# A ring of ten weight places in place of nine, filled in running order, and a turn of ten expert bodies in place of three

## The chip, the cores and the metric

The kernel runs on one core of one Trainium2 chip. The metric is the device time of one execution in microseconds, as the median of several runs. Three runs of the kernel before took 1612.6, 1609.94 and 1607.69 us; their median is 1609.94 us.

## The reference, cut to what matters

Two layers work on 512 tokens of 1,024 float32 values. Layer 0 mixes with a four-head retention, layer 1 with a Conformer convolution (a first pointwise product with gating, a depthwise convolution of width 31, a norm, a second pointwise product). After each mixer comes a mixture of experts, and this part is the one that the change is about: 32 experts in four groups, each token goes to the two best experts of its best group.

```python
def run_block(args):
    xblk, e = args
    return (jax.nn.silu(xblk @ w_gate[e]) * (xblk @ w_up[e])) @ w_down[e]
```

Gate and up are 1024 x 512, down is 512 x 1024, so an expert has 6 MB of float32 weights and a layer's 32 experts have 192 MB. Every expert of a layer is read once from memory, whichever tokens it gets. The output is x plus the weighted sum over a token's two experts.

## The kernel before, in words

All five engines run programs of their own that meet at semaphores. TensorE does all products. The token rows of an expert are gathered in blocks of 32 rows (BLK); the blocks of all experts stand in one row, expert after expert, and an expert has at least one block. The number of blocks up to an expert is known only on the chip and stands in the table `cum`.

Weights come in loads of 2 MB, which are 16 KB for each of the 128 partitions. An expert is three such loads: gate and up for the first half of the model's width (w_gu0), the same for the second half (w_gu1), and down (w_down). Their places in on-chip memory are the six slots of `ring` and three areas that serve other stages too: place 6 is in area_c, place 7 in area_b, place 8 is hT (lines 215 and 216). Slots 4 and 5 hold, outside the expert stages, the split weight tiles w_hi and w_lo and hT_lo (lines 152 to 154), so they come free late.

Before, the nine places are three sets of three (`slots_of`, line 283): expert e uses set e mod 3, and its three loads always go to the same places of that set. All loads are issued from SyncE (SP), in program order, each on a wait that tells that the place is free:

- `first_experts` (lines 337 to 348) loads experts 0 and 1 of layer 0 into slots 0 to 5 as the last retention head lets go of them: one load each after the last three groups of eight weight tiles and after the last one (`lo_ready`), then two more after `tile_used`. Places 6 and 7 follow at once (lines 357, 358), and place 8 after the router's first product has read hT (`logitT_mm`, line 359). That is nine loads.
- The stream (lines 366 to 386) issues the other 87 loads of the layer: w_gu0 of expert e once the first half of gate and up of all blocks of expert e - 3 is computed (`gu_half`), w_gu1 at `gu_mm`, w_down at `y_mm`. Nine turns of a hardware loop cover experts 3 to 29, with the source address in a register; experts 30 and 31 are written out.
- Behind the stream of layer 0 come four loads of the convolution's first product (w_pw1, slots 0 to 3, lines 389 to 397) and two of its second (w_pw2, slots 0 and 1), then nine loads of layer 1's experts (lines 404 to 417 and 360), again each behind the wait that frees its place.

TensorE's side is `experts` (line 848): a loop of ten turns with three expert bodies each, one for every set of places, then experts 30 and 31 written out. Each body holds an inner loop over the expert's blocks, `with pe.Fori(first, after) as t`, whose bounds are read from `cum`. `one_block` (line 814) waits for w_gu0's load, does 16 matmuls (line 826; the profile counts two for each, 32), adds rows of the block before (`put_rows`, line 809), waits for w_gu1's load, does as many again, gathers rows of the next block (`pick_rows`, line 762), and after the down load does 16 more (line 843). The waits for the loads are

```python
pe.wait_ge(slot_loaded[s], 16 * turn + (expert_base(l, s) + 16))
```

and the same for s_down. ScalarE (line 540), GpSimd (line 445) and VectorE (line 1230) have loops of their own over all blocks, which the diff leaves as they are.

Of the kernel before, what the change touches and what calls it, by code (L numbers as in the profile page):

```python
# [29 lines left out]
P = 128  # L30
# [9 lines left out]
NE = NG * NPG  # L40
# [6 lines left out]
NBLK = 72  # L47
BIG = 1.0e6
FAR = 1.0e30
SLOT = 4096  # L50
NSLOT = 6
NWT = 4
# [10 lines left out]
DEPTH = 3  # L63
LOOPED = NE // DEPTH * DEPTH
# [29 lines left out]
def program(nc, x_in, pos_in, const_in, decay_in, par_in, w_qk, w_v, w_g, w_out, w_pw1, w_pw2, b_pw2,  # L94
            w_router, b_router, w_gu0, w_gu1, w_down, g_final, tok_in, out):
    with ExitStack() as ctx:
# [47 lines left out]
        aT_e = sb("aT_e", [P, P])  # L144

        def over(name, shape, under, words):
# [69 lines left out]
            [area_c[:, 0:SLOT], area_b[:, 0:SLOT], hT[:, :, :].rearrange("p k s -> p (k s)")]  # L216
# [4 lines left out]
        slot_loaded = sems("slot_loaded", 3 * DEPTH)  # L221
# [34 lines left out]
        sig_ready, u_ready, z_ready, mean_mm, centred, squared, var_ready, var_mm, lnroot_ready, zn_ready, \  # L256
            zh_ready, pw2_mm, x2_added, pad_zero, dve_conv = (
                sem(n) for n in ("sig_ready", "u_ready", "z_ready", "mean_mm", "centred", "squared", "var_ready", "var_mm",
# [3 lines left out]
        def both(name):  # L262
            return sems(name, NL)
        wts_ready, rstd_ready, logitT_ready, logitT_mm, logit_mm, exp_arg, exp_ready, onehot_ready, rank_mm, cum_ready, spread_ready, idx_mm, idx_ready = (
            both(n) for n in ("wts_ready", "rstd_ready", "logitT_ready", "logitT_mm", "logit_mm", "exp_arg", "exp_ready", "onehot_ready", "rank_mm", "cum_ready",
# [20 lines left out]
        in_conv = [32, 32, 16, 16, 0, 0, 0, 0, 0]  # L286
# [18 lines left out]
        def _(sp):  # L305
# [31 lines left out]
            def first_experts(l, tiles):  # L337

                sources = [(w_gu0, 0), (w_gu1, 0), (w_down, 0), (w_gu0, 1), (w_gu1, 1), (w_down, 1)]
                for s, (w, e) in enumerate(sources):  # L340
                    if s < 4:
                        sp.wait_ge(lo_ready, tiles[s])
                    elif s == 4:

                        sp.wait_ge(tile_used, NWT + tiles[4])
                    load_slot(s, w[l, e])

            first_experts(0, [ret_tiles - n * TILES for n in (3, 2, 1, 0, 0)])

            for l in range(NL):  # L350
                gu0_l = w_gu0[l].rearrange("e p c -> (e p) c")
                gu1_l = w_gu1[l].rearrange("e p c -> (e p) c")
                down_l = w_down[l].rearrange("e p c -> (e p) c")

                if l == 0:

                    load_slot(6, w_gu0[l, 2])
                    load_slot(7, w_gu1[l, 2])
                sp.wait_ge(logitT_mm[l], 1)
                load_slot(8, w_down[l, 2])  # L360
                sp.wait_ge(cum_ready[l], 1)
                sp.wait_ge(idx_mm[l], 1)
                sp.dma_start(tok_number, tok_in.partition_broadcast(P)).then_inc(tok_loaded[l], 16)
                if l == 1:
                    sp.dma_start(gfin, g_final.partition_broadcast(P)).then_inc(gfin_loaded, 16)
                with sp.Fori(1, LOOPED // DEPTH) as turn:
                    for n in range(DEPTH):
                        s_gu0, s_gu1, s_down = slots_of[n]

                        upto = sp.value_load(cum[0:1, bass.ds(DEPTH * turn + (n - 2), 1)], min_val=1, max_val=NBLK - 1)  # L370
                        e = DEPTH * turn + n
                        sp.wait_ge(gu_half[l], upto)
                        load_slot(s_gu0, gu0_l[bass.ds(e * P, P), :])
                        sp.wait_ge(gu_mm[l], upto)
                        load_slot(s_gu1, gu1_l[bass.ds(e * P, P), :])
                        sp.wait_ge(y_mm[l], upto)
                        load_slot(s_down, down_l[bass.ds(e * P, P), :])
                for e in range(LOOPED, NE):
                    s_gu0, s_gu1, s_down = slots_of[e % DEPTH]
                    upto = sp.value_load(cum[0:1, e - 2:e - 1], min_val=1, max_val=NBLK - 1)  # L380
                    sp.wait_ge(gu_half[l], upto)
                    load_slot(s_gu0, w_gu0[l, e])
                    sp.wait_ge(gu_mm[l], upto)
                    load_slot(s_gu1, w_gu1[l, e])
                    sp.wait_ge(y_mm[l], upto)
                    load_slot(s_down, w_down[l, e])
                if l == 0:

                    total = sp.value_load(cum[0:1, NE:NE + 1], min_val=NE, max_val=NBLK - 1)
                    last = sp.value_load(cum[0:1, NE - 1:NE], min_val=1, max_val=NBLK - 1)  # L390
                    for j in range(4):
                        if j == 2:

                            sp.wait_ge(y_mm[l], last)
                        else:
                            sp.wait_ge(gu_mm[l], last if j < 2 else total)
                        load_slot(j, w_pw1[j])
                if l == 0:
# [26 lines left out]
        def _(pool):  # L425
            def split_lo(n, place, s, at):

                pool.wait_ge(hi_ready, n + 1)
                nc.gpsimd.tensor_tensor(w_lo[:, place, :], ring[:, s, at:at + 512],  # L429
                                        w_hi[:, place, :].bitcast(F32), ALU.subtract).then_inc(lo_ready, 1)  # L430
# [7 lines left out]
            for l in range(NL):  # L438
                if l == 1:
                    for n in range(pw1_tiles + 2 * TILES):  # L440
                        split_lo(ret_tiles + n, n % NWT, n // TILES % 4, tile_column(False, n % TILES))
# [15 lines left out]
        def _(act):  # L457
# [10 lines left out]
            def split_hi(n, place, s, at):  # L468

                act.wait_ge(tile_used, n + 1)  # L470
                nc.scalar.copy(w_hi[:, place, :], ring[:, s, at:at + 512]).then_inc(hi_ready, 1)  # L471
# [148 lines left out]
            def split_conv(first, last):  # L620
                for n in range(first, last):
                    if n % TILES == 0:
                        s = n // TILES % 4

                        act.wait_ge(slot_loaded[s], expert_base(1, s) - in_conv[s] + (16 if n < pw1_tiles else 32))
                    split_hi(ret_tiles + n, n % NWT, n // TILES % 4, tile_column(False, n % TILES))
# [62 lines left out]
        def _(pe):  # L689
# [124 lines left out]
            def one_block(l, t, turn, s_gu0, s_gu1, s_down):  # L814

                gate_up = [places[s].rearrange("p (k w f) -> p k w f", k=KT // 2, w=2) for s in (s_gu0, s_gu1)]
                down = places[s_down].rearrange("p (k d) -> p k d", k=4)
                pe.wait_ge(hgT_ready[l], t + 1)  # L820
                for n, (s, done) in enumerate(((s_gu0, gu_half), (s_gu1, gu_mm))):

                    pe.wait_ge(slot_loaded[s], 16 * turn + (expert_base(l, s) + 16))
# [16 lines left out]
                pe.wait_ge(slot_loaded[s_down], 16 * turn + (expert_base(l, s_down) + 16))  # L840
# [7 lines left out]
            def experts(l):  # L848
                with pe.Fori(0, LOOPED // DEPTH) as turn:
                    for n in range(DEPTH):  # L850
                        slots = slots_of[n]
                        if n == 0:
                            first = pe.value_load(cum[0:1, bass.ds(DEPTH * turn, 1)], min_val=0, max_val=NBLK - 2)
                        else:
                            first = after
                        after = pe.value_load(cum[0:1, bass.ds(DEPTH * turn + (n + 1), 1)], min_val=1, max_val=NBLK - 1)
                        with pe.Fori(first, after) as t:
                            one_block(l, t, turn, *slots)
                for e in range(LOOPED, NE):
                    first = pe.value_load(cum[0:1, e:e + 1], min_val=0, max_val=NBLK - 2)  # L860
                    after = pe.value_load(cum[0:1, e + 1:e + 2], min_val=1, max_val=NBLK - 1)
                    with pe.Fori(first, after) as t:
                        one_block(l, t, e // DEPTH, *slots_of[e % DEPTH])
# [684 lines left out]
```

## Time and profile before

| what | value |
|---|---|
| median of three runs | 1609.94 us |
| the profiled execution: its span, first to last instruction | 1607.4 us |
| a time of its own beside that span | not given; the lowest of the three runs is 1607.69 us |
| TensorE busy | 1491.0 us, 93% |
| VectorE busy | 999.4 us, 62% |
| moved by DMA | 457.63 MB, mean 285 GB/s |
| chain that ended last | TensorE 72%, DMA 21%, VectorE 4% |

The page gives busy times over the whole span. The expert stages lie at about 464 to 912 us and 1138 to 1592 us, and in them and in the other stages different things limit the time, so the page's totals are read stage by stage.

### The profile page before, as it was taken

The page shows a single profiled execution, that of the slowest core. Times are in us where ns is not written, and L with a number is a line of the kernel's source. Part 1 is how long each engine was busy: PE and PEld are TensorE (multiplying, and loading weights), DVE is VectorE, ACT ScalarE, POOL GpSimd, SP SyncE. Part 2 cuts the span into 40 slices and gives each one's busy share as a digit, 9 for nine tenths or more (in the row PEclk, how much of TensorE's full clock was granted, in tenths as well). Part 3 has the DMA queues.
Part 4 walks back from the last instruction along what each step waited for, and adds up shares of the span by engine and source line. Part 5 has one row for each costly group of instructions (what it writes and reads, how often), then busy time and mean ns, then how long its engine had stood idle before and what let it go on. Part 6 is the DMA issues. An engine that isn't in the chain of part 4 may idle for free.

```text
span 1607.4 us, 45636 instructions
## 1 busy us (share of the span) xinstructions
PE 1491.0 (93%) x19098; PEld 980.1 (61%) x19099; DVE 999.4 (62%) x1665; ACT 447.4 (28%) x734; POOL 399.6 (25%) x368
## 2 busy tenths in 40 slices
PE   8999999999989999997789899989999999889996
PEld 6868778687645555554445588667555555445553
DVE  5122112220378888785667889973888877668877
ACT  5242422322432222221112342154122222112222
POOL 4434344244102212111111255112112111111211
PEclk9999999999999999999999999999999999999999
DMA  9212112122289999999999711126399999999995
GB/s 380 106 53 95 63 60 99 53 105 105 85 368 427 429 429 428 429 429 429 427 429 429 336 61 45 55 105 274 123 429 426 429 429 428 429 429 428 428 429 250
DMA packets 33995, 457.63 MB, mean 285 GB/s; under 512 B 3856, under 2 KB 3984, under 8 KB 6544
## 3 DMA queue, kind: packets, MB, share of 16 engines
q1 hardware_dynamic: 33792, 456.57, 68.0%
q8 instruction: 48, 0.79, 0.2%
q10 hardware_dynamic: 144, 0.18, 0.0%
q14 instruction: 11, 0.09, 0.0%
HBM read 454.64 MB, written 2.10 MB: 284 GB/s over the span
## 4 chain that ended last, share of the span: by engine, by line
PE 72%; DMA 21%; DVE 4%; issue 2%; ACT 1%; POOL 0%; DVEq 0%; SPq 0%; ACTq 0%
PE ps L826 14%; DMA hT<-w_down 14%; PE ps L717 10%; PE ps L718 10%; PE ps L719 10%; PE ps L843 8%; PE ps L762 7%; PE ps L809 5%; DMA ring<-w_down 4%; DMA ring<-w_gu 3%; PE ps L991 2%; PE ps L911 2%; PE ps L903 1%; DVE x L1224 1%; PE ps L772 0%
## 5 line engine op out<-in xcount | busy, mean ns | idle before, releaser
L1224 DVE TENSOR_TENSOR x<-x,ps 128x1024 f32<-128x1024 f32 x384 | 451.1, 1216 | 85.8 <-PE ps L809 85.8
L429 POOL TENSOR_TENSOR w_lo<-ring,w_hi 128x512 fp32r<-128x512 f32 x176 | 235.1, 1338 | 384.1 <-ACT w_hi L471 384.0
L452 POOL TENSOR_SCALAR slot_tok<-trig,slot_now 128x512 fp32r<-128x512 f32 x94 | 147.0, 1564 | 711.6 <-PE ps L809 711.6
L826 PE MATMUL ps<-ring,hgT 128*32 128x256 f32 x4160 | 263.3, 395 | 50.6 <-DMA ring<-w_gu 29.7
L826 PEld LDWEIGHTS ps<-ring,hgT 128*32 128x32 f32 x4160 | 130.1, 112 | 151.4 <-issue 44.6
L471 ACT CAST w_hi<-ring 128x512 fp32r<-128x512 f32 x176 | 109.1, 625 | 339.7 <-PE ps L719 339.7
L762 PE MATMUL ps<-area_a,block_rows 128*32 128x256 f32 x3072 | 184.9, 381 | 0.6 <-DVE block_rows L1186 0.6
L545 ACT ACTIVATE y_hi<-ps,slots 128x256 fp32r<-128x256 f32 x94 | 44.8, 476 | 392.8 <-PE ps L843 392.8
L762 PEld LDWEIGHTS ps<-area_a,block_rows 128*32 128x32 f32 x3072 | 101.0, 111 | 69.7 <-issue 5.6
L843 PE MATMUL ps<-ring,aT_e 128*32 128x256 f32 x2080 | 125.7, 382 | 2.7 <-DMA ring<-w_down 2.6
L717 PE MATMUL ps<-w_hi,hT_hi 128*128 128x512 f32 x320 | 125.1, 391 | 3.0 <-DVE hT_lo L1442 1.7
L809 PEld LDWEIGHTS ps<-y_hi,slot_tok 32*128 32x128 f32 x1536 | 74.1, 183 | 84.6 <-issue 80.8
L718 PE MATMUL ps<-w_lo,hT_hi 128*128 128x512 f32 x320 | 124.5, 389 | 0.0
L719 PE MATMUL ps<-w_hi,hT_lo 128*128 128x512 f32 x320 | 124.5, 389 | 0.0
L809 PE MATMUL ps<-y_hi,slot_tok 32*128 32x256 f32 x1536 | 121.2, 330 | 2.8 <-DVE y_lo L1245 2.8
L542 ACT ACT_TABLE_LOAD x94 | 120.6, 1283 | 10.8 <-DVEq L1220 9.2
L542 ACT ACTIVATE sg_e<-ps 128x128 f32<-128x128 f32 x94 | 26.1, 278 | 315.4 <-PE ps L826 315.4
L717 PE MATMUL ps<-hT_hi,w_hi 128*128 128x512 f32 x256 | 100.2, 391 | 1.3 <-DVE hT_lo L1068 0.9
L809 PE MATMUL ps<-y_lo,slot_tok 32*128 32x256 f32 x1536 | 100.6, 276 | 0.0
L719 PE MATMUL ps<-hT_hi,w_lo 128*128 128x512 f32 x256 | 99.6, 389 | 0.0
L718 PE MATMUL ps<-hT_lo,w_hi 128*128 128x512 f32 x256 | 99.6, 389 | 0.0
L843 PEld LDWEIGHTS ps<-ring,aT_e 128*32 128x32 f32 x2080 | 61.9, 109 | 44.4 <-issue 3.5
(234 smaller groups left out, 1921.6 us busy)
## 6 DMA issues: line engine op xcount, KB each, us to landing
ring<-w_gu SPq DMA_DIRECT2D x88, 2048.0 KB, 28.8
ring<-w_down SPq DMA_DIRECT2D x44, 2048.0 KB, 29.8
area_c<-w_gu SPq DMA_DIRECT2D x20, 2048.0 KB, 30.2
area_b<-w_gu SPq DMA_DIRECT2D x20, 2048.0 KB, 32.8
hT<-w_down SPq DMA_DIRECT2D x20, 2048.0 KB, 33.4
ring<-w_pw SPq DMA_DIRECT2D x6, 2048.0 KB, 11.6
ring<-w_v SPq DMA_DIRECT2D x4, 2048.0 KB, 9.1
ring<-w_g SPq DMA_DIRECT2D x4, 2048.0 KB, 8.4
```

What stands on the lines that cost most here:

```text
L429: nc.gpsimd.tensor_tensor(w_lo[:, place, :], ring[:, s, at:at + 512], w_hi[:, place, :].bitcast(F32), ALU.subtract).then_inc(lo_ready, 1)
L452: nc.gpsimd.tensor_scalar(slot_tok[:, :], tok_number, slot_now[:, 0:1], None, ALU.is_equal).then_inc(tok_hot[l], 1)
L471: nc.scalar.copy(w_hi[:, place, :], ring[:, s, at:at + 512]).then_inc(hi_ready, 1)
L542: nc.scalar.activation(sg_e[:, :], ps[:, 2, 0:P], ACT.Silu).then_inc(silu_ready[l], 1)
L717: nc.tensor.matmul(at, lhs[0], rhs[0], start=start, stop=False)
L718: nc.tensor.matmul(at, lhs[0], rhs[1], start=False, stop=False)
L719: return nc.tensor.matmul(at, lhs[1], rhs[0], start=False, stop=stop)
L762: last = nc.tensor.matmul(ps[32 * g:32 * g + 32, 0, 0:QW], block_rows[:, i, :], xn[:, i, g * QW:(g + 1) * QW], start=(i == 0), stop=(i == ...
L809: last = nc.tensor.matmul(ps[:, bank + g, i * QW:(i + 1) * QW], slot_tok[rows, cols], part[rows, :], start=(i == 0 and n == 0), stop=(i == ...
L826: last = nc.tensor.matmul(ps[32 * g:32 * g + 32, 2, 0:256], hgT[:, n * (KT // 2) + k, :], gate_up[n][:, k, :, g * P:(g + 1) * P], start=(n ...
L843: last = nc.tensor.matmul(ps[32 * g:32 * g + 32, 3, P:P + QW], aT_e[:, k * BLK:(k + 1) * BLK], down[:, k, g * 256:(g + 1) * 256], start=(k ...
L1224: return V.tensor_tensor(x[:, i, :].rearrange("p (g c) -> p g c", g=4), x[:, i, :].rearrange("p (g c) -> p g c", g=4), ps[:, bank:bank + 4 ...
```

## The change

The ring gets a tenth place, `spare`, a tensor of its own of 16 KB for each partition. To make room for it the memory set aside for DMAs with dynamic descriptors is set to 1,024 bytes in the call that makes the program. The 96 loads of a layer are numbered in the order of use, n = 3e for w_gu0, 3e + 1 for w_gu1, 3e + 2 for w_down, and load n goes to the place `FILL[l][n % 10]`. `FILL` lists the places in the order in which they come free ahead of each layer. Ten loads are issued ahead of the stream, and the stream issues loads 10 to 95, load n on the wait that tells that load n - 10 was used. The ten loads of layer 0 are: load 0 into the spare place right behind the last retention head's w_out, loads 1 to 4 on the same four waits as before, loads 5 to 8 behind `tile_used`, load 9 after `logitT_mm`. SyncE's stream is no loop any more but 86 loads written out for each layer. On TensorE a turn holds ten expert bodies (ten experts take thirty loads, after which the places repeat); three turns and two bodies written out make 32. The convolution's six loads go to places 9, 0, 1, 2 and 3, 9; the first w_pw2 load follows the w_pw1 loads at once. Unused semaphores are dropped.

```diff
-DEPTH = 3
-LOOPED = NE // DEPTH * DEPTH
+NPLACE = 10
+LOADS = 3 * NE
+TURN_E = 10
+LOOPED = NE // TURN_E * TURN_E
+
+FILL = ((9, 0, 1, 2, 3, 6, 4, 7, 5, 8), (0, 1, 2, 6, 7, 3, 9, 4, 5, 8))
...
+        spare = sb("spare", [P, SLOT])
...
-            [area_c[:, 0:SLOT], area_b[:, 0:SLOT], hT[:, :, :].rearrange("p k s -> p (k s)")]
+            [area_c[:, 0:SLOT], area_b[:, 0:SLOT], hT[:, :, :].rearrange("p k s -> p (k s)"), spare[:, :]]
...
-        after_ret = [64, 64, 64, 64, 0, 0, 0, 0, 0]
+        after_ret = [64, 64, 64, 64, 0, 0, 0, 0, 0, 0]
+
+        in_conv = [16, 16, 16, 16, 0, 0, 0, 0, 0, 32]
+
+        def after_first(s):
+
+            return after_ret[s] + 16 * len(range(FILL[0].index(s), LOADS, NPLACE))
 
         def expert_base(l, s):
 
-            experts = len(range(s // 3, NE, DEPTH))
-            return after_ret[s] + l * (16 * experts + in_conv[s])
-
-
-        slots_of = [(0, 1, 2), (3, 4, 5), (6, 7, 8)]
...
+            return after_first(s) + in_conv[s] if l else after_ret[s]
+
+
+        pw1_place = (9, 0, 1, 2)
+        pw2_place = (3, 9)
...
+            def load_expert(l, n):
+
+                w = (w_gu0, w_gu1, w_down)[n % 3]
+                load_slot(FILL[l][n % NPLACE], w[l, n // 3])
+
+            def stream(l):
+
+                upto = None
+                for n in range(NPLACE, LOADS):
+                    e, part = (n - NPLACE) // 3, (n - NPLACE) % 3
+                    if part == 0:
+                        upto = sp.value_load(cum[0:1, e + 1:e + 2], min_val=1, max_val=NBLK - 1)
+                        sp.wait_ge(gu_half[l], upto)
+                    elif part == 1:
+                        sp.wait_ge(gu_mm[l], upto)
+                    else:
+                        sp.wait_ge(y_mm[l], upto)
+                    load_expert(l, n)
+
+            load_expert(0, 0)
+            for n in range(1, 5):
+                sp.wait_ge(lo_ready, ret_tiles - (4 - n) * TILES)
+                load_expert(0, n)
+            sp.wait_ge(tile_used, NWT + ret_tiles)
+            for n in range(5, 9):
+                load_expert(0, n)
...
                 sp.wait_ge(logitT_mm[l], 1)
-                load_slot(8, w_down[l, 2])
+                load_expert(l, 9)
...
-                with sp.Fori(1, LOOPED // DEPTH) as turn:
-                    for n in range(DEPTH):
-                        s_gu0, s_gu1, s_down = slots_of[n]
...
+                stream(l)
                 if l == 0:
...
+                    sp.wait_ge(gu_half[l], last)
+                    load_slot(pw1_place[0], w_pw1[0])
+                    sp.wait_ge(gu_mm[l], last)
+                    load_slot(pw1_place[1], w_pw1[1])
+                    sp.wait_ge(y_mm[l], last)
+                    load_slot(pw1_place[2], w_pw1[2])
+                    sp.wait_ge(gu_half[l], total)
+                    load_slot(pw1_place[3], w_pw1[3])
+                    sp.wait_ge(gu_mm[l], total)
+                    load_slot(pw2_place[0], w_pw2[0])
+
+                    split = ret_tiles + pw1_tiles
+                    sp.wait_ge(lo_ready, ret_tiles + TILES)
+                    load_slot(pw2_place[1], w_pw2[1])
                     for n in range(2):
-                        sp.wait_ge(lo_ready, ret_tiles + (n + 1) * TILES)
-                        load_slot(n, w_pw2[n])
-                    split = ret_tiles + pw1_tiles
-
+                        sp.wait_ge(lo_ready, ret_tiles + (n + 2) * TILES)
+                        load_expert(1, n)
                     sp.wait_ge(lo_ready, split)
-                    load_slot(3, w_gu0[1, 1])
                     sp.wait_ge(conv_mm, ROUNDS)
-                    load_slot(2, w_down[1, 0])
+                    load_expert(1, 2)
                     sp.wait_ge(hTlo_ready, 3 * KT)
-                    load_slot(6, w_gu0[1, 2])
-                    load_slot(7, w_gu1[1, 2])
-                    sp.wait_ge(lo_ready, split + TILES)
-                    load_slot(0, w_gu0[1, 0])
-                    sp.wait_ge(lo_ready, split + 2 * TILES)
-                    load_slot(1, w_gu1[1, 0])
+                    load_expert(1, 3)
+                    load_expert(1, 4)
+                    for n in range(2):
+                        sp.wait_ge(lo_ready, split + (n + 1) * TILES)
+                        load_expert(1, 5 + n)
                     sp.wait_ge(tile_used, NWT + split + 2 * TILES)
-                    load_slot(4, w_gu1[1, 1])
-                    load_slot(5, w_down[1, 1])
+                    load_expert(1, 7)
+                    load_expert(1, 8)
...
-            def one_block(l, t, turn, s_gu0, s_gu1, s_down):
+            def one_block(l, t, turn, e):
...
+                s_gu0, s_gu1, s_down = (FILL[l][(3 * e + n) % NPLACE] for n in range(3))
+                arrived = [16 * ((3 * e + n) // NPLACE + 1) for n in range(3)]
...
-                    pe.wait_ge(slot_loaded[s], 16 * turn + (expert_base(l, s) + 16))
+                    pe.wait_ge(slot_loaded[s], 48 * turn + (expert_base(l, s) + arrived[n]))
...
-                with pe.Fori(0, LOOPED // DEPTH) as turn:
-                    for n in range(DEPTH):
-                        slots = slots_of[n]
+                with pe.Fori(0, LOOPED // TURN_E) as turn:
+                    for n in range(TURN_E):
...
                         with pe.Fori(first, after) as t:
-                            one_block(l, t, turn, *slots)
+                            one_block(l, t, turn, n)
...
-    nc = bacc.Bacc("TRN2", target_bir_lowering=False, num_devices=1)
+    nc = bacc.Bacc("TRN2", target_bir_lowering=False, num_devices=1, dynamic_dma_scratch_size=1024)
```

## Rows read from the trace of the kernel before

**Rows 1.** The page: span, TensorE, DMA share by 40 slices, instruction queue

```profile
span 1607.4 us, 45636 instructions
...
PE 1491.0 (93%) x19098; PEld 980.1 (61%) x19099; DVE 999.4 (62%) x1665; ACT 447.4 (28%) x734; POOL 399.6 (25%) x368
...
DMA  9212112122289999999999711126399999999995
...
q8 instruction: 48, 0.79, 0.2%
```

**Rows 2.** DMA in the stretches 501 to 875 us and 1240 to 1580 us

```profile
DMA packets 11000, 160.29 MB, mean 429 GB/s; under 512 B 1217, under 2 KB 1217, under 8 KB 1217
...
q1 hardware_dynamic: 11000, 160.29, 100.7%
...
DMA packets 9999, 145.72 MB, mean 429 GB/s; under 512 B 1105, under 2 KB 1105, under 8 KB 1105
```

**Rows 3.** Waits for loads: first five rows 468 to 912 us, then 1138 to 1592 us

```profile
PE ps L826 <- DMA ring<-w_gu: 19.2, 9, 2.9
PE ps L826 <- DMA area_c<-w_gu: 4.9, 2, 2.9
PE ps L826 <- DMA area_b<-w_gu: 3.4, 3, 1.9
PE ps L843 <- DMA hT<-w_down: 2.3, 4, 0.7
PE ps L843 <- DMA ring<-w_down: 1.3, 2, 0.6
...
PE ps L826 <- DMA ring<-w_gu: 10.5, 6, 2.7
PE ps L826 <- DMA area_c<-w_gu: 5.7, 2, 2.9
```

**Rows 4.** Chain of waits, the last load each layer waited for: start us, us

```profile
884.41 1.93 PE ps L843 x32
...
1512.68 26.86 DMA ring<-w_gu
1539.58 3.58 PE ps L826 x32
```

**Rows 5.** SyncE's issues at the start of layer 0's stream: start us, us

```profile
437.72 0.43 SPq L308 DMA_DIRECT2D ring<-w_down  x1
...
445.13 0.33 SPq L308 DMA_DIRECT2D hT<-w_down  x1
...
468.23 2.75 SPq L308 DMA_DIRECT2D ring<-w_gu  x2
474.91 0.33 SPq L308 DMA_DIRECT2D ring<-w_down  x1
```

**Rows 6.** DMA, us to landing of the loads issued at 470.64 and 474.91 us

```profile
ring<-w_gu SPq DMA_DIRECT2D x1, 2048.0 KB, 11.0
...
ring<-w_down SPq DMA_DIRECT2D x1, 2048.0 KB, 13.0
```

**Rows 7.** Instruction queue, 468.5 to 500.5 us; then a retention turn, either one

```profile
q8 instruction: 3, 0.05, 0.6%
...
q8 instruction: 8, 0.13, 0.3%
```

**Rows 8.** Busy time by stretch: one retention turn (two heads), one expert block

```profile
13.50:225.50 212.00, 207.81 (x878) 161.25 (x876) 59.41 (x95) 78.03 (x137) 87.01 (x67) 1.00 0.31 120
474.60:483.20 8.60, 8.60 (x168) 4.97 (x160) 7.31 (x13) 2.04 (x3) 1.82 (x3) 1.00 1.00 427
```

**Rows 9.** Chain of waits where a turn ends: experts at 500 us, heads at 225 us

```profile
500.55 1.03 issue
501.58 1.93 PE ps L826 x32
...
225.40 0.40 issue
```

More of the change, by code:

```diff
@@ L255, in program @@
             sem(n) for n in ("diag_ready", "held_ready", "conv_mm", "zv_ready", "half_mm", "half_ready", "shift_mm", "shift_ready", "shifted", "squared_v", "sums_mm", "mean_known", "mean_ready", "scale_known", "scale_mm"))
-        sig_ready, u_ready, z_ready, mean_mm, centred, squared, var_ready, var_mm, lnroot_ready, zn_ready, \
+        sig_ready, u_ready, z_ready, mean_mm, centred, squared, var_ready, lnroot_ready, zn_ready, \
             zh_ready, pw2_mm, x2_added, pad_zero, dve_conv = (
-                sem(n) for n in ("sig_ready", "u_ready", "z_ready", "mean_mm", "centred", "squared", "var_ready", "var_mm",
+                sem(n) for n in ("sig_ready", "u_ready", "z_ready", "mean_mm", "centred", "squared", "var_ready",
                                  "lnroot_ready", "zn_ready", "zh_ready", "pw2_mm", "x2_added", "pad_zero",
@@ L263, in both @@
             return sems(name, NL)
-        wts_ready, rstd_ready, logitT_ready, logitT_mm, logit_mm, exp_arg, exp_ready, onehot_ready, rank_mm, cum_ready, spread_ready, idx_mm, idx_ready = (
-            both(n) for n in ("wts_ready", "rstd_ready", "logitT_ready", "logitT_mm", "logit_mm", "exp_arg", "exp_ready", "onehot_ready", "rank_mm", "cum_ready",
+        rstd_ready, logitT_ready, logitT_mm, logit_mm, exp_arg, exp_ready, onehot_ready, rank_mm, cum_ready, spread_ready, idx_mm, idx_ready = (
+            both(n) for n in ("rstd_ready", "logitT_ready", "logitT_mm", "logit_mm", "exp_arg", "exp_ready", "onehot_ready", "rank_mm", "cum_ready",
                               "spread_ready", "idx_mm", "idx_ready"))
@@ L365, in _ @@
                     sp.dma_start(gfin, g_final.partition_broadcast(P)).then_inc(gfin_loaded, 16)
-                with sp.Fori(1, LOOPED // DEPTH) as turn:
-                    for n in range(DEPTH):
-                        s_gu0, s_gu1, s_down = slots_of[n]
[L370 to L386, printed above, removed]
+                stream(l)
                 if l == 0:
@@ L390, in _ @@
                     last = sp.value_load(cum[0:1, NE - 1:NE], min_val=1, max_val=NBLK - 1)
[L391 to L398, printed above, removed]
+                    sp.wait_ge(gu_half[l], last)
+                    load_slot(pw1_place[0], w_pw1[0])
@@ L428, in split_lo @@
                 pool.wait_ge(hi_ready, n + 1)
-                nc.gpsimd.tensor_tensor(w_lo[:, place, :], ring[:, s, at:at + 512],
+                nc.gpsimd.tensor_tensor(w_lo[:, place, :], places[s][:, at:at + 512],
                                         w_hi[:, place, :].bitcast(F32), ALU.subtract).then_inc(lo_ready, 1)
@@ L470, in split_hi @@
                 act.wait_ge(tile_used, n + 1)
-                nc.scalar.copy(w_hi[:, place, :], ring[:, s, at:at + 512]).then_inc(hi_ready, 1)
+                nc.scalar.copy(w_hi[:, place, :], places[s][:, at:at + 512]).then_inc(hi_ready, 1)
             def norm_hi(n, m, gain, tiles=range(KT)):
@@ L839, in one_block @@
                 pe.wait_ge(aT_ready[l], t + 1)
-                pe.wait_ge(slot_loaded[s_down], 16 * turn + (expert_base(l, s_down) + 16))
+                pe.wait_ge(slot_loaded[s_down], 48 * turn + (expert_base(l, s_down) + arrived[2]))
                 for k in range(4):
@@ L848, in experts @@
             def experts(l):
-                with pe.Fori(0, LOOPED // DEPTH) as turn:
-                    for n in range(DEPTH):
-                        slots = slots_of[n]
+                with pe.Fori(0, LOOPED // TURN_E) as turn:
+                    for n in range(TURN_E):
                         if n == 0:
-                            first = pe.value_load(cum[0:1, bass.ds(DEPTH * turn, 1)], min_val=0, max_val=NBLK - 2)
+                            first = pe.value_load(cum[0:1, bass.ds(TURN_E * turn, 1)], min_val=0, max_val=NBLK - 2)
                         else:
                             first = after
-                        after = pe.value_load(cum[0:1, bass.ds(DEPTH * turn + (n + 1), 1)], min_val=1, max_val=NBLK - 1)
+                        after = pe.value_load(cum[0:1, bass.ds(TURN_E * turn + (n + 1), 1)], min_val=1, max_val=NBLK - 1)
                         with pe.Fori(first, after) as t:
-                            one_block(l, t, turn, *slots)
+                            one_block(l, t, turn, n)
                 for e in range(LOOPED, NE):
@@ L862, in experts @@
                     with pe.Fori(first, after) as t:
-                        one_block(l, t, e // DEPTH, *slots_of[e % DEPTH])
+                        one_block(l, t, 0, e)
                 total = pe.value_load(cum[0:1, NE:NE + 1], min_val=NE, max_val=NBLK - 1)
```

26 lines of the change are left out of this document (5 added, 21 removed).

## The prediction

> **What bounds the kernel now.** I read the page first, then one stage at a time. The page's totals name TensorE, 93% busy, with the DMA queues full only in two long stretches [rows 1]. The totals mislead here: they average stages with different limits. The row of DMA digits shows 9s in slices 12 to 23 and 30 to 40, which are the two expert stages. Inside them, from 501 to 875 us and from 1240 to 1580 us, the core moves 429 GB/s without a break [rows 2]. A load is 2,048 KB, 2.10 MB, so it takes 2.10 MB / 429 GB/s = 4.89 us. There are 87 stream loads in a layer, 87 x 4.89 = 425 us of the roughly 430 us from the first stream issue at 468.23 us [rows 5] to the last landing. A TensorE block takes 8.60 us [rows 8], and the trace has 47 blocks in each layer (94 in both), 404 us. So the DMA stream is longer than TensorE's own work by some 20 us, and TensorE waits for loads: 31.1 us in layer 0 (five rows) and at least 16.2 us in layer 1 (two rows) [rows 3]. The last such wait ends at 884.41 us for a down load in layer 0, and at 1539.58 us for a gate and up load in layer 1 [rows 4]. Behind those two points TensorE runs on its own to the layer's end, so whatever moves the landing moves the end with it.
>
> **Step 1, one load less in each stream.** Ten loads stand ready instead of nine, so 86 are streamed instead of 87. That is only worth something if the tenth is loaded in time that the DMAs have free. They have it: load 0 goes into the spare place behind the last w_out, at about 322 us, where the DMA digits stand at 0 to 2 [rows 1]. From about 437 us on the same loads are issued before and after (four, the row at 437.72 us is the second, and then hT's at 445.13 us), and the stream begins at 468.23 us with the same wait, half of gate and up of expert 0 [rows 5]. The k-th stream load waits for the use of load k in both kernels, so the DMAs never get their work later than before. In layer 1 two loads go early, into places 0 and 1 while the convolution's first product runs, where one went before. From 1078 us on the number of issues is the same. Each landing from the tenth on then comes one load time earlier: -4.89 us for each layer, -9.8 us for both.
>
> Does TensorE follow? Let it be s ahead of its old times. At a wait of length w for a load that lands 4.89 us earlier, it is then min(s + w, 4.89) ahead. In stretches where it does not wait, it keeps s. The waits add up to 31 and at least 16 us, far over 4.89, before the last ones [rows 3, 4], so it takes all of it.
>
> **Step 2, ten bodies in a turn.** This has a saving and a price. The saving: each turn of three ends in 1.03 us of issue [rows 9]. Nine such jumps in a layer become two, 7 x 1.03 = 7.2 us less TensorE time. It is worth nothing, since the loads' landings hide it; if they did not, it would be the gain.
>
> The price is code. A block is 160 weight loads and as many matmuls (168 matmul records touch that stretch) [rows 8], 320 instructions. A retention turn has 878 with 876, 1,754 instructions [rows 8], and it is fetched anew in both turns, 8 packets each [rows 7]. A turn of three expert bodies has 960, and of the nine turns that follow the first the long stretch shows none: from 501 to 875 us all 11,000 packets are the weight queue's [rows 2]. So a loop of 960 instructions stays in TensorE's store and one of 1,754 does not. A turn of ten bodies has 3,200: it will not stay, and every body of it is fetched again. At 8 packets for 1,754 that is 1.46 a body, 32 x 1.46 = 47 packets a layer where about 6 came before.
>
> What does a packet cost when the DMAs are full? The page gives 48 packets 0.2% of 16 engines' span, 0.002 x 16 x 1607.4 / 48 = 1.1 us each [rows 1]. On the stream itself I can see one: the load issued at 470.64 us lands after 11.0 us at 481.6, the next one, issued at 474.91, after 13.0 us at 487.9 [rows 6]. That is 6.3 us where 4.9 is the step, 1.3 to 1.4 us more, in the stretch with three instruction packets [rows 7]. A load is complete when its slowest DMA engine is, so only packets on the engine furthest behind count. Three packets cost the stream one packet's time, so they went to different engines. If packets go round the 16 engines, 47 / 16 = 2.9, so the slowest is hit three times instead of once: 2 x 1.35 = 2.7 us a layer. Bounds: nothing (packets always land on engines with time to spare) and 47 x 1.35 / 3, 21 us, less the 1.35 paid now, 20 us (all of them cost as the first three did). I take 2.7, nearer to the row that shows different engines than to either end. SyncE's stream is now written out too, 86 loads of two to four instructions in place of a short loop. That is one or two packets more, 0.2 us. So step 2 costs 2.9 us a layer, 5.8 us in both.
>
> The Trainium skill speaks against charging this. "Runtime: NRT & Kernel Launch", section "Instruction fetch mechanics", says that TensorE has 128 KiB of instruction store, filled in blocks of 256 instructions, and that crossing a block is mostly hidden. By that rule the cost would be zero and the sum -9.8 us, the first rival below. Its sizes agree with what the rows show (960 stays, 1,754 spills with look-ahead).
>
> **Step 3, the jump back to missing code.** Twice a layer the turn jumps 3,200 instructions back. The trace has no such jump into code that is surely gone. From below: 0.40 us at the heads' jump [rows 9]. From above: a packet that queues like a load behind two others, 13 us [rows 6]. I take 3 us, as for one packet with its way there and back. It is hidden: the jumps come before experts 10 and 20, TensorE has gained 7 us on boundaries, and in both layers it waits for loads around and after expert 20. Nothing on the path.
>
> **Step 4, all the rest.** The convolution's loads are issued relative to the layer's last blocks, one wait earlier each, and move along. The first w_pw2 load comes earlier into idle time. Waits have new constants only. The smaller descriptor memory touches no queue in use, since loads go out from SyncE. Nothing.
>
> **Sum.** -9.8 + 5.8 = -4.0 us against the profiled execution, whose span is 1607.4 us. The median of the runs shown, 1609.94 us, is 2.5 us over that span. A difference carries over: 1609.94 - 4.0 = 1605.9 us. A measurement can tell about 0.3%, 4.8 us, from no change.
>
> **Rivals.**
> 1. The fetches hide, and all 9.8 us stay: 1600.1 us. For it: no TensorE stall shows in the first turn while packets come, and only one of three cost the stream anything. Against it: that one cost 1.3 us. The runtime page's rule named above stands behind it. Chance 0.25.
> 2. Slower: the fetches bunch on the engine that is furthest behind. Place: the landing of the last load that TensorE waits for. Price: 1.35 us a hit. It decides from 4.89 / 1.35 = 3.6 hits more than now in a layer. With six hits in place of one it is 6.8 - 4.9 = +1.9 a layer, +3.7 us, 1613.6 us. With eight, +4.6 a layer, 1619 us. At the upper bound, 20 us a layer, it would be 1640 us. For it: the one visible hit fell on the slowest engine among only three packets. Against it: three packets, one hit. Chance 0.20.
> 3. The change doesn't do what it says: a load of the ten is late, or the ring runs dry at the layer's start, and the stream gains no load time. Then only step 2's cost is left, 1615.7 us. Against it: the equal issues in [rows 5]. Chance 0.05.
>
> **How the numbers follow.** My forecast, 1603 to 1608 us, has 0.50. The range of 8 in 10 takes it in, goes down to 1599.5 for rival 1 and up to 1617 for most of rivals 2 and 3. Faster by over 4.8 us: rival 1 and the lower third of my own case (two hits on the slowest engine instead of three), 0.25 + 0.15 = 0.40. Within 4.8 us: the rest of my case and the mild end of rival 2, 0.42. Slower: 0.18. Both signs are possible; the likeliest case alone is 1603 to 1608.
>
> **What would show it.** Right: 429 GB/s still held in both stages; first stream issue at the same distance from the stage's start; the instruction queue at about 120 packets or more in place of 48, with packets all through both stages; steps between landings of 4.9 us with a few of about 6.3; the last waited-for landing 1 to 3 us earlier in each layer; one 1.03 us issue gap per ten experts. Rival 1: the same packets but landings a full 4.9 us earlier. Rival 2: five or more long steps in a layer. Wrong altogether: DMA digits below 9 inside a stage, or new TensorE waits for issue behind the last load wait.

## The result: 0.36% slower, and the profile after

Five runs of the changed kernel took 1614.57 to 1615.98 us, median 1615.03 us, against 1609.94 us before. The ratio is 1.0036, 95% interval [1.0023, 1.0048]. A later round, 11 runs of the same kernel, gave 1.0025 [1.0015, 1.0034]. I had forecast 1605.9 us: the time fell inside my range, on the other side of no change.

The page of the kernel after (answers to [rows 1]):

```profile
span 1613.0 us, 45258 instructions
...
PE 1492.2 (93%) x19098; PEld 978.6 (61%) x19099; DVE 998.7 (62%) x1665; ACT 446.6 (28%) x734; POOL 399.9 (25%) x368
...
DMA  9212112142289999999999812026299999999995
...
q8 instruction: 126, 2.06, 0.5%
```

TensorE did the same work, 19,098 matmuls in 1492.2 us. The instruction queue went from 48 packets to 126.

DMA of the kernel after in the stretch 501 to 875 us (answers to [rows 2]):

```profile
DMA packets 10945, 159.39 MB, mean 426 GB/s; under 512 B 1216, under 2 KB 1216, under 8 KB 1216
...
q1 hardware_dynamic: 10904, 158.73, 100.0%
q8 instruction: 39, 0.64, 0.7%
q14 instruction: 2, 0.02, 0.0%
```

Where every packet was a weight packet before, there are now 39 instruction packets, and the weights moved are 158.73 MB instead of 160.29. That is 1.56 MB less, or 1.56 / 429 GB/s = 3.6 us of stream, while the instructions are only 0.64 MB.

SyncE's issues at the start of layer 0's stream, kernel after (answers to [rows 5]):

```profile
439.94 0.33 SPq L316 DMA_DIRECT2D area_c<-w_down  x1
...
447.72 0.33 SPq L316 DMA_DIRECT2D hT<-w_gu  x1
...
470.65 0.33 SPq L316 DMA_DIRECT2D spare<-w_gu  x1
473.18 0.33 SPq L316 DMA_DIRECT2D ring<-w_down  x1
```

The tenth load was in place, as step 1 said: from the load into hT to the first stream issue it is 22.9 us, before it was 23.1. (All times are 2.4 to 2.6 us late here. That comes from the retention stage, see the last experiment.)

Each load raises its semaphore by 16, one for each DMA engine, and the trace keeps the time of each. The table gives, for the first and the last of a layer's loads in the stream, when each of the 16 parts had landed, in us from the first of them, sorted, and last the landing of the whole load. The trace does not name the engine of a part.

```
before, layer 0
0.00 0.08 0.08 0.12 0.13 0.15 0.20 0.21 0.22 0.23 0.24 0.25 0.61 0.82 1.49 1.60   476.67
0.00 0.02 0.03 0.05 0.09 0.12 0.16 0.19 0.20 0.64 0.75 1.56 1.68 1.70 2.04 2.96   898.96
after, layer 0
0.00 0.09 0.11 0.12 0.16 0.16 0.22 0.23 0.24 0.36 0.38 0.38 0.60 0.61 0.80 1.01   478.59
0.00 0.06 0.08 0.24 0.26 0.40 0.64 1.50 7.56 7.85 8.01 8.65 9.23 9.27 9.31 9.80   903.29
after, layer 1
0.00 0.01 0.08 0.11 0.13 0.15 0.16 0.19 0.21 0.26 0.28 0.28 0.77 0.91 1.05 1.12  1170.84
0.00 0.07 0.12 0.14 0.73 0.78 0.94 1.02 7.77 7.77 7.86 8.91 9.31 9.38 9.44 9.49  1595.02
```

This is the result in one picture. Eight of the sixteen parts end 7.6 to 9.8 us behind the fastest, the other eight stay within 1.5 us. I read from this that the instruction packets of the stream went through eight engines, about evenly. From 478.59 to 903.29 us in layer 0 the lags add up to 67.4 us more, over 44 large packets and two of half the size: 1.5 us a packet. Four engines with five packets and four with six make 44, and five or six times 1.5 us is 7.5 or 9 us, as in the table. A load has landed when its slowest engine is done.

The sum: from the first stream landing to the last it took 422.3 us with 87 loads before (476.67 to 898.96) and 424.7 with 86 after. Layer 1: 421.9 before, 424.2 after. It splits in two. The fastest engine took 420.9 us before in both layers, and 415.9 and 415.8 after: 4.89 us a load each time, so it never stood still and one load less is worth 5.0 us. The slowest engine's lag on it grew within the stream by 1.35 and 1.03 us before, by 8.8 and 8.4 after, that is by 7.4 and 7.3 us more. So the last landing loses 2.4 and 2.3 us against the first.

The program does not get all of that. From the first stream issue of layer 0 to that of layer 1 it took 689.9 us before and 692.2 after, +2.3. From there to layer 1's last product it took 433.4 and 434.3, only +0.8: before, TensorE waited for its last load at 1539.58 us and ended 3.1 us behind the last landing; after, it waits for that landing and ends 2.1 us behind it. In these two traces the expert stages and what lies between them thus account for 3.1 us, and the remaining 2.4 of the 5.6 us between the spans arise before the first stream issue. The medians differ by 5.1 us in one round and by 3.8 in the other. What makes up the 1 to 2 us between 3.1 and these is not shown; the last experiment says what is known of it.

Waits for loads of the kernel after, 470 to 917 us (answers to [rows 3]):

```profile
PE ps L824 <- DMA ring<-w_gu: 13.5, 6, 3.0
PE ps L824 <- DMA area_c<-w_gu: 4.2, 2, 2.3
PE ps L824 <- DMA spare<-w_gu: 2.4, 2, 1.7
PE ps L841 <- DMA ring<-w_down: 1.7, 2, 1.0
```

and its chain of waits at the first jump back in layer 0, at the second, and at the last load wait of either layer (answers to [rows 4, 9]):

```profile
587.35 1.86 PE ps L841 x32
589.22 7.00 issue
596.21 2.78 PE ps L824 x23
...
729.72 7.24 issue
736.96 2.78 PE ps L824 x23
...
883.72 0.04 issue
883.77 3.40 PE ps L824 x32
...
1565.28 29.73 DMA ring<-w_down
1595.02 0.14 issue
1595.15 1.97 PE ps L841 x32
```

TensorE waits 7.0 and 7.2 us where the turn jumps back; I read it as the wait for the code of the turn's first body. Each wait also costs clock: a stretch at 1.2 GHz of 6.8 to 10.2 us begins within each of the four. For the first jump, in 589 to 604 us, where the third number from the end is the granted clock:

```profile
589.00:604.00 15.00, 7.15 (x73) 3.13 (x72) 3.65 (x7) 1.76 (x2) 0.28 (x2) 0.66 1.02 430
```

Behind the second jump it still waits for loads up to 883.77 us, and the fastest DMA engine never stood still, so the jumps are hidden: their time is taken out of load waits. In layer 1 the last load of all, at 1595.02 us, is now waited for.

### The profile page after: what moved, and what is told of

Same layout as the page of the kernel before. It is cut to its first block, busy times and chain, and to the rows that moved or that the text cites. A ratio compares the mean times of both kernels' runs of the same rounds, so it can differ in the third digit from the quotient of the medians.

```text
span 1613.0 us, 45258 instructions
## 1 busy us (share of the span) xinstructions
PE 1492.2 (93%) x19098; PEld 978.6 (61%) x19099; DVE 998.7 (62%) x1665; ACT 446.6 (28%) x734; POOL 399.9 (25%) x368
## 4 chain that ended last, share of the span: by engine, by line
PE 77%; DMA 15%; DVE 4%; issue 3%; ACT 1%; POOL 0%; DVEq 0%; SPq 0%; ACTq 0%
PE ps L824 17%; PE ps L713 10%; PE ps L715 10%; PE ps L714 10%; PE ps L841 8%; PE ps L758 8%; PE ps L805 6%; DMA ring<-w_gu 6%; DMA spare<-w_down 5%; DMA spare<-w_gu 2%; PE ps L988 2%; PE ps L908 2%; DMA ring<-w_down 2%; PE ps L900 1%; PE ps L768 0%
## 5 line engine op out<-in xcount | busy, mean ns | idle before, releaser
L425 POOL TENSOR_TENSOR w_lo<-ring,w_hi 128x512 fp32r<-128x512 f32 x160 | 213.4, 1336 | 359.5 <-ACT w_hi L467 359.5
L824 PE MATMUL ps<-ring,hgT 128*32 128x256 f32 x3616 | 229.4, 396 | 39.1 <-DMA ring<-w_gu 21.4
L824 PEld LDWEIGHTS ps<-ring,hgT 128*32 128x32 f32 x3616 | 112.8, 113 | 126.8 <-issue 38.7
L467 ACT CAST w_hi<-ring 128x512 fp32r<-128x512 f32 x160 | 99.0, 623 | 320.1 <-PE ps L715 320.1
L841 PE MATMUL ps<-ring,aT_e 128*32 128x256 f32 x1696 | 103.8, 382 | 5.9 <-issue 3.8
L1102 DVE STREAM_TRANSPOSE hg<-ps 128x256 f32<-128x256 f32 x96 | 43.2, 450 | 71.0 <-PE ps L758 71.0
```

The source lines that it names most:

```text
L425: nc.gpsimd.tensor_tensor(w_lo[:, place, :], places[s][:, at:at + 512], w_hi[:, place, :].bitcast(F32), ALU.subtract).then_inc(lo_ready, 1)
L467: nc.scalar.copy(w_hi[:, place, :], places[s][:, at:at + 512]).then_inc(hi_ready, 1)
L824: last = nc.tensor.matmul(ps[32 * g:32 * g + 32, 2, 0:256], hgT[:, n * (KT // 2) + k, :], gate_up[n][:, k, :, g * P:(g + 1) * P], start=(n ...
L841: last = nc.tensor.matmul(ps[32 * g:32 * g + 32, 3, P:P + QW], aT_e[:, k * BLK:(k + 1) * BLK], down[:, k, g * 256:(g + 1) * 256], start=(k ...
```

## The experiments

My theory from this profile was: the extra packets sit on eight engines, cost 1.5 us each there, and nothing else matters. The rivals were moved memory, SyncE's written-out stream, the order of the places, a tenth load that gains nothing, and the 7 us jumps.

**Only the memory moved.**

```diff
+        spare = sb("spare", [P, SLOT])
...
-    nc = bacc.Bacc("TRN2", target_bir_lowering=False, num_devices=1)
+    nc = bacc.Bacc("TRN2", target_bir_lowering=False, num_devices=1, dynamic_dma_scratch_size=1024)
```

> The kernel before with only the spare tensor allocated (never used) and the descriptor memory cut to 1,024 bytes, so that what lies in on-chip memory moves as in the change. In the changed kernel's profile the retention stage lost 2.5 us to two 3.4 us stretches at the lower TensorE clock. If these came by chance: 1609.9 us, within 0.1%. If moved memory or the smaller descriptor memory causes them: about 1612.5 us (+0.15%), with the lower clock at about 98 and 204 us in the profile.

Measured: 1609.02 us against 1609.78, ratio 0.9995 [0.9986, 1.0004]. Moved memory and the smaller descriptor memory cost nothing that these runs could tell, and the streams took 422.4 and 422.1 us, as before.

**Nine bodies in the turn, nothing else changed.**

```diff
+BODIES = 9
...
-                    pe.wait_ge(slot_loaded[s], 16 * turn + (expert_base(l, s) + 16))
+                    pe.wait_ge(slot_loaded[s], 16 * each * turn + (expert_base(l, s) + 16 + 16 * more))
...
-                with pe.Fori(0, LOOPED // DEPTH) as turn:
-                    for n in range(DEPTH):
-                        slots = slots_of[n]
+                with pe.Fori(0, NE // BODIES) as turn:
+                    for n in range(BODIES):
+                        slots = slots_of[n % DEPTH]
...
-                            one_block(l, t, turn, *slots)
-                for e in range(LOOPED, NE):
+                            one_block(l, t, turn, *slots, each=BODIES // DEPTH, more=n // DEPTH)
+                for e in range(NE // BODIES * BODIES, NE):
```

> The kernel before, nine places, but nine expert bodies in TensorE's turn (three turns, five bodies written out). Theory (instruction packets on eight of the sixteen DMA engines, 1.55 us each): about 44 instruction packets inside each stream instead of 5, spread over eight engines, 5.5 each; the last landing comes 6.8 us later in each layer, no load time is gained, so +13.6 us, 1623.5 us. Rival (the price lies in the order of places or in SyncE's written-out stream, not in TensorE's code): no change, 1610 us. My forecast's price for code, 2.7 us a layer: 1615.3 us.

Measured: 1625.48 us, ratio 1.009 [1.0077, 1.0104], +15.7 us. The queues from the first issue of layer 0's stream to its last landing, nine bodies:

```profile
q1 hardware_dynamic: 12649, 184.31, 99.4%
q8 instruction: 44, 0.72, 0.7%
```

The same 87 loads took 429.8 and 429.4 us, 7.5 and 7.4 us longer than before. At the last load of each stream eight parts end 7.7 to 10.2 us behind, eight within 1.2, and the fastest engine again took 4.89 us a load. With nine places and with SyncE's loop untouched, TensorE's code alone costs what the theory says and 2 us more. From the first stream issue to layer 1's last product the trace has 12.9 us more than before; the other 3.4 of the 16.2 us between the two spans lie ahead of it, where this trace too has two stretches at 1.2 GHz.

**A tenth load, used once, with the loop of three bodies kept.** Spare holds w_gu0 of expert 3; the slot that it would have taken gets w_gu0 of expert 6, the first load of the stream.

```diff
+            load_slot(9, w_gu0[0, 3])
             first_experts(0, [ret_tiles - n * TILES for n in (3, 2, 1, 0, 0)])
...
-                with sp.Fori(1, LOOPED // DEPTH) as turn:
+                for e in range(DEPTH, 3 * DEPTH):
+                    s_gu0, s_gu1, s_down = slots_of[e % DEPTH]
+                    upto = sp.value_load(cum[0:1, e - 2:e - 1], min_val=1, max_val=NBLK - 1)
+                    sp.wait_ge(gu_half[l], upto)
+                    if e != 2 * DEPTH:
+                        load_slot(s_gu0, w_gu0[l, 2 * DEPTH if e == DEPTH else e])
...
+                with sp.Fori(3, LOOPED // DEPTH) as turn:
...
+                for e in range(FIRST):
...
+                        one_block(l, t, e // DEPTH, 9 if e == DEPTH else s_gu0, s_gu1, s_down)
+                with pe.Fori(0, (NE - FIRST) // DEPTH) as turn:
```

> The kernel before with a tenth load ready ahead of each stream, kept in the spare place, used once (w_gu0 of expert 3), and TensorE's loop of three bodies kept: experts 0 to 4 written out, then nine turns of three. SyncE writes out experts 3 to 8 and loops over the rest. Theory: 86 loads in place of 87 in each stream, -4.9 us each, against at most one more instruction packet on the slowest engine, 0 to 1.5 us: 1600 to 1603 us. Rival (a tenth load gains nothing, because something else than the stream's length sets the end): 1610 us or more.

Measured: 1599.93 us against 1609.78, ratio 0.994 [0.9927, 0.9954], -9.8 us. It beats both kernels. Together with nine bodies' +15.7 it gives +5.9, where the change measured +5.1 and +3.8: that leaves the order of the places, which no run varied alone, no cost to explain. Its page, the queue in layer 0's stream, and its waits for loads in that layer:

```profile
span 1598.0 us, 45595 instructions
```

```profile
q1 hardware_dynamic: 12476, 181.87, 100.3%
q8 instruction: 10, 0.16, 0.2%
```

```profile
PE ps L844 <- DMA ring<-w_gu: 15.0, 8, 2.9
PE ps L844 <- DMA area_b<-w_gu: 5.7, 3, 2.3
PE ps L844 <- DMA area_c<-w_gu: 4.9, 3, 2.9
PE ps L861 <- DMA ring<-w_down: 3.3, 5, 0.7
```

The streams took 419.0 and 419.5 us with 86 loads, 3.3 and 2.4 us less than before, with 10 and 9 packets in them in place of 5. So the tenth load is worth what step 1 said, less a packet or so on the slowest engine, whose lag grew by 3.0 and 3.1 us in place of 1.35 and 1.03. The difference in spans, 9.4 us, is more than the streams' 5.7. The rest is not in the stretch between the stages (0.4 us longer here): the stream began 1.5 us earlier in this profile, its first loads landed 0.8 and 0.9 us sooner after their issue, and TensorE ended 1.0 us closer behind the last landing. How much of that belongs to the kernel one trace can't say.

**Only SyncE's stream written out.**

```diff
-                with sp.Fori(1, LOOPED // DEPTH) as turn:
...
-                for e in range(LOOPED, NE):
+                for e in range(DEPTH, NE):
```

> The kernel before with SyncE's stream of loads written out for all 29 experts in place of its loop; TensorE as before. Theory: SyncE needs only one or two instruction packets more a layer; no change, 1609.9 us, at most +0.5. Rival (SyncE's code costs as much as TensorE's): 1615 us or more.

Measured: 1609.57 us, ratio 0.9997 [0.9988, 1.0006]. It costs nothing that these runs could tell. Its streams took 422.4 and 422.2 us, as before.

**The tenth load with no code added.** Spare holds w_gu0 of expert 1, whose slot takes that of expert 4 ahead of the stream. Two bodies in front and ten turns of three are five bodies, as many as before.

```diff
-                sources = [(w_gu0, 0), (w_gu1, 0), (w_down, 0), (w_gu0, 1), (w_gu1, 1), (w_down, 1)]
+                sources = [(w_gu0, 0), (w_gu1, 0), (w_down, 0), (w_gu0, 4), (w_gu1, 1), (w_down, 1)]
...
+            load_slot(9, w_gu0[0, 1])
...
+FIRST = 2
```

> As the kernel with the tenth load used once, but with no more code than the kernel before: the spare place holds w_gu0 of expert 1, so its slot can take w_gu0 of expert 4 ahead of the stream; experts 0 and 1 are written out in front, and ten turns of three bodies do experts 2 to 31. Theory: 86 loads in each stream, and 5 or fewer instruction packets in it, none of them late: the full 4.9 us a layer or a little more, 1597 to 1600 us, 0 to 2.5 us under the kernel with eight bodies of code. Rival (the packets were not what separated that kernel from the full gain): the same time as that kernel, 1599.9 us.

Measured: 1601.27 us (1596.62 to 1604.92), ratio 0.9944 [0.9925, 0.9963]. It is not told apart from the kernel before it, 0.994, so the gain that I expected over it did not show. In the profile the streams took 419.7 and 417.8 us, 2.6 and 4.2 less than before, with 6 and 5 instruction packets in them. The lag of the slowest engine grew by no more than before, 0.8 and 1.0 us, so the packets are not what keeps the gain under 4.9. The fastest engine too lost time: 3.0 us in layer 0, at one load. It had finished the load before at 496.27 us, and this one was issued at 497.34:

```profile
486.13 0.33 SPq L310 DMA_DIRECT2D ring<-w_down  x1
497.34 0.33 SPq L310 DMA_DIRECT2D area_c<-w_gu  x1
```

The stream ran dry at the layer's start, because a place came free too late for a stream that was now one load further on; the same thing cost 0.8 us once in layer 1. That is the place of my third rival, in this kernel and not in the changed one, where the fastest engine kept to 4.89 us a load.

**Six bodies in the turn.** The same edit with `BODIES = 6`.

> The kernel before with six expert bodies in TensorE's turn (five turns, two bodies written out), 1,920 matmul and weight load instructions and some 100 others a turn. Theory (any loop that the store doesn't hold is fetched whole in every turn, as the heads' 1,754 are): about as many packets in the streams as with nine bodies, 44, +13 to +15 us, 1624 us, and the jumps back cost under 1 us in place of 7, since the target is still there. Rival (the price grows with the length of the turn, or comes from the 7 us jumps): clearly less, 1615 us or under.

Measured: 1626.44 us, ratio 1.0099 [1.0083, 1.0115], +16.6 us. The packets came as expected, the jumps did not. The queue in layer 0's stream, and the chain at the first jump back, six bodies:

```profile
q8 instruction: 48, 0.79, 0.7%
```

```profile
526.43 1.86 PE ps L844 x32
528.29 7.17 issue
535.47 2.78 PE ps L827 x23
```

With six bodies the jump waits 7.17 us too, so the target was not there any more. The eight such jumps of the program, four a layer, wait 6.9 to 7.4 us each, and now they are not all hidden. The streams took 432.9 and 429.9 us. Of the 10.6 and 7.9 us over before, the slowest engine's lag makes 5.6 and 5.2; the rest, 5.0 and 2.8 us, the fastest engine lost too, at loads that were issued only after it had run out of work (at 647.64 and 664.75 us in layer 0, at 1524.33 in layer 1). In layer 1 TensorE waits for no load behind 1442.41 us, so the jump at 1495.79 us, 6.96 us, lies on the path in full. That the total equals that of nine bodies is therefore partly chance: the same number of packets, less lag, and jumps that show.

The loop of 960 matmuls and weight loads is free of fetches, and the heads' 1,754 and this one's 1,920 are fetched in every turn, so for packets it does not matter how long the turn is beyond that: each body is fetched once in every pass.

**The changed kernel again.**

> The changed kernel once more, for a second profile. If the two stretches at the lower TensorE clock in the retention stage came by chance, they need not be there again, and the stage is up to 2.5 us shorter in this profile; the streams' durations, 424.7 and 424.2 us from the first to the last landing, are the same within 0.3 us. Median 1615 us.

Measured: 1613.57 us, ratio 1.0025 [1.0015, 1.0034]. Busy times in the stretches 70 to 100 and 190 to 215 us, where the column behind the five engines is the granted TensorE clock, first in the first profile of the changed kernel, then in this one:

```profile
70.00:100.00 30.00, 27.94 (x107) 18.74 (x106) 8.26 (x16) 13.88 (x27) 6.39 (x5) 0.97 0.20 71
190.00:215.00 25.00, 22.95 (x83) 15.18 (x82) 6.29 (x12) 13.49 (x26) 4.56 (x4) 0.93 0.00 1
```

```profile
70.00:100.00 30.00, 27.94 (x109) 18.69 (x108) 7.81 (x16) 14.10 (x27) 6.39 (x5) 1.00 0.20 71
190.00:215.00 25.00, 22.95 (x89) 15.23 (x89) 6.47 (x13) 13.66 (x27) 5.12 (x4) 1.00 0.00 1
```

The same program, with TensorE busy for the same 27.94 and 22.95 us, has two stretches at 1.2 GHz in one execution and none in the other, and the span is 1613.0 in the one and 1609.2 us in the other. So the 2.4 us by which everything was late before the expert stage need not come with the change. A third stretch of 3.4 us, at 1142.8 us between the expert stages, is there in the first profile and missing in the second; layer 1's first stream issue comes 1.6 us sooner after layer 0's last product in the second. Other kernels' traces have two such early stretches (nine bodies, six bodies, the tenth load with no code added), one (SyncE's stream written out) or none, among them kernels with little code and with much. Whether the longer code makes them more frequent, and so explains why the medians differ by 5.1 and 3.8 us where the stages show 3.1 here and 1.8 in the second profile, these traces can't tell. The streams took 424.6 and 424.2 us here, as in the first profile. That part repeats.

## Why the prediction was wrong

- **Step 1, one load less, -4.89 us a layer: right.** The tenth load came in free time, the stream kept its start, the fastest engine ended 5.0 us sooner in each layer, and the kernels with a tenth load and three bodies show a gain, 1599.93 and 1601.27 us.
- **Step 2, the number of packets: right.** I said 47 a layer, the trace shows 44 in each stream, and 126 in the page. That a turn of ten bodies is fetched anew followed from the heads' loop. Of the store's size the runs show only that a loop of 960 stays and that 1,754 and 1,920 do not. The saving of turn ends was hidden, as said.
- **Step 2, what the packets cost: here the prediction failed.** The term "if packets go round the 16 engines, 47 / 16 = 2.9, so the slowest is hit three times instead of once: 2 x 1.35 = 2.7 us a layer" had the right mechanism and was too small on two counts. The landings show eight engines that are hit, 44 / 8 = 5.5, and 1.5 us a packet, not 1.35. The lag grew by 7.4 and 7.3 us a layer in place of 2.7. With -5.0 that gives +2.4 and +2.3 instead of -2.2. I had taken three packets that went to different engines as a sign for sixteen. Three packets can't tell eight from sixteen, and the landings of the 16 parts of each load were in the trace. I had used only the last of them.
- **The signs.** I expected a few steps of about 6.3 us between landings. None came: 17 steps in layer 0 and 11 in layer 1 were over 5.2 us, the longest 5.7 and 6.0. The rival's sign, five or more long steps in a layer, came in this form. I read it so that the engines take turns at being furthest behind, and each packet adds a part of its 1.5 us.
- **From landing to end: not one to one.** I wrote that whatever moves the last waited-for landing moves the end with it. Before, layer 1's last landing was not waited for, and TensorE ended 3.1 us behind it; now it ends 2.1 us behind it, so layer 1 passed on 1.0 us less than its stream lost.
- **The rule that I weighed against it.** "Runtime: NRT & Kernel Launch", section "Instruction fetch mechanics", of the Trainium skill says that crossing a block is mostly hidden. For TensorE that held: inside a turn of the changed kernel no matmul waits longer than 1.4 us where the profile shows nothing to wait for. The traces show that the cost falls on the weight queue instead, 7 us a layer.
- **Step 3, the jump back: 7.0 to 7.2 us, not 3, and hidden as said.** The same section of the Trainium skill says that a taken branch to a target outside the two pages it holds stalls until the target's page is fetched. The traces agree for the long turns, with 7.0 us here. They do not for the loop of 960, which is longer than two pages of 256 instructions: its jump back takes 1.03 us, with no instruction packet in the stretch [rows 2, 9]. With six bodies, four such jumps a layer, it is no longer all hidden.
- **SyncE's own packets, 0.2 us: too small to measure,** ratio 0.9997.
- **Rival 2 was the one that came**, close to its milder figure: "six hits in place of one ... +1.9 a layer". Its mechanism was off too: the packets did not bunch on one engine, they spread about evenly over half of them. I gave it 0.20. The sign hung on one number, the count of engines, with break-even at 3.6 hits more, and I should have given the two sides nearly equal chances.

## What to carry to other kernels

Where a DMA stream is the limit, TensorE's code is traffic in it. Before unrolling a loop, count its body against what a trace shows to stay (here 960 matmuls and weight loads stayed, 1,754 did not), since a loop that does not stay is fetched again in every pass, and find out over how many engines the packets spread: here it was eight of sixteen. A place more in a ring is worth up to one load time of a saturated stream, if the places still come free in time. It can be had without touching the ring's period: use it once, ahead of the stream, and leave the loop as it is. To see such a loss, take the 16 parts of a load's landing instead of the bandwidth: 429 against 426 GB/s looks like nothing. The first part tells whether the stream ran dry, the last how far the slowest engine lags.

## What the runs showed of the hardware that I had not expected

- The 44 instruction packets of a stream delayed eight of the 16 parts of a load and not the others: eight end 7.6 to 9.8 us behind in the changed kernel, 7.7 to 10.2 with nine bodies, and the other eight stay within 1.5 us.
- Each costs its engine about 1.5 us of weight transfer while the queues are full, though the page's share puts such a packet at 0.005 x 16 x 1613 / 126 = 1.0 us.
- A jump back to code that is fetched again takes 6.7 to 7.4 us with full DMA queues in 18 of the 20 such jumps of these traces, and 11.1 and 11.2 us in the two of layer 1 with nine bodies. A loop of 960 matmul and weight load instructions stays, one of 1,920 does not, and its first body is gone as well. The heads' loop of 1,754 is fetched again too, but its jump took 0.40 us.
- Within the wait at each of the changed kernel's four jumps TensorE's granted clock fell to 1.2 GHz, for 6.8 to 10.2 us (0.66 in 589 to 604 us).
- The same program in two executions has or has not two stretches at 1.2 GHz in its first 220 us, with TensorE busy for the same time in both.
